# Order of the even mixer's projection and of its gates, a place of its own for the attention output, and new plans for two side jobs

## What is computed

```python
def even_mixer(x, w_in, w_out, lam_params, sub_g, lb, hg_g, lam_init, cos, sin):
    h = x @ w_in
    qa, ka, va, hq, hf, hi, hg = jnp.split(h, cuts, axis=-1)
    o_a = diff_attention(qa, ka, va, lam_params, sub_g, lam_init, cos, sin)
    o_b = hgrn2(hq, hf, hi, hg, lb, hg_g)
    return jnp.concatenate([o_a, o_b], axis=-1) @ w_out

def hgrn2(hq, hf, hi, hg, lb, out_g):
    q = silu(hq); f = lb + (1 - lb) * sigmoid(hf); kk = 1 - f
    ...
    o = o_intra + o_inter
    return rms_norm(o, out_g) * silu(hg)

def second_block(x, c, ctx, c_ctx, w_mod, b_mod, ...):
    mod = s_lat @ w_mod[i] + b_mod[i]        # per layer, needs no x
    mod_c = s_ctx @ w_mod[i] + b_mod[i]
```

## Time and profile before

| what | value |
|---|---|
| median of 3 runs | 1862.49 us (1861.61 to 1865.78) |
| the profiled execution | 1861.59 us, span 1860.3 us |
| TensorE (PE) busy | 1791.5 us, 96% |
| VectorE (DVE) busy | 1274.8 us, 69% |
| ScalarE (ACT) busy | 990.7 us, 53% |
| HBM read | 331.55 MB, 179 GB/s over the span |
| mean granted TensorE clock | 0.987 |

### The profile page before, as it was taken

One profiled execution on the slowest core, in us unless ns is written; L12 is line 12 of the kernel. 1 busy time (PEld: TensorE's weight loads), 2 busy tenths in 40 slices (PEclk: granted clock), 3 DMA queues, 4 the chain that ended last, 5 costly groups with the idle time before them and its releaser, 6 DMA issues. The chain is left out here.

```text
span 1860.3 us, 35694 instructions
## 1 busy us (share of the span) xinstructions
PE 1791.5 (96%) x14792; PEld 1666.0 (90%) x14792; DVE 1274.8 (69%) x2351; ACT 990.7 (53%) x1740; POOL 77.5 (4%) x78
## 2 busy tenths in 40 slices
PE   7999999999999999999999999999999999989997
PEld 6877799978988999999899988899999888779997
DVE  5556566667778855876666777766667867876665
ACT  4563544455656644654665655544456564644443
POOL 0000100020000100000200101000001000100000
PEclk9999999999999999999999999999999999999999
DMA  9878866765434465455454443455555543235653
GB/s 377 307 269 315 327 187 189 223 223 164 132 130 133 155 187 188 131 164 182 138 172 159 144 163 103 148 165 181 188 193 185 167 136 103 81 120 185 183 185 121
DMA packets 93825, 334.92 MB, mean 180 GB/s; under 512 B 10960, under 2 KB 12880, under 8 KB 93536
## 3 DMA queue, kind: packets, MB, share of 16 engines
q1 hardware_dynamic: 92016, 327.33, 53.9%
q0 software_dynamic: 1648, 5.31, 0.9%
HBM read 331.55 MB, written 1.05 MB: 179 GB/s over the span
## 5 line engine op out<-in xcount | busy, mean ns | idle before, releaser
L565 DVE TENSOR_TENSOR low<-ring,high 128x1024 fp32r<-128x1024 f32 x410 | 503.6, 1229 | 218.8 <-ACT high L557 206.7
L590 PE MATMUL bank<-XHx,high 128*128 128x256 f32 x2096 | 609.5, 291 | 26.1 <-DVE low L565 10.0
L591 PE MATMUL bank<-XLx,high 128*128 128x256 f32 x2096 | 593.7, 283 | 0.0
L592 PE MATMUL bank<-XHx,low 128*128 128x256 f32 x2096 | 592.8, 283 | 0.0
L557 ACT CAST high<-ring 128x1024 fp32r<-128x1024 f32 x410 | 428.4, 1046 | 280.8 <-PE bank L592 227.7
L590 PEld LDWEIGHTS bank<-XHx,high 128*128 128x128 f32 x2096 | 399.8, 191 | 42.9 <-issue 18.3
L591 PEld LDWEIGHTS bank<-XLx,high 128*128 128x128 f32 x2096 | 400.3, 191 | 1.3
L592 PEld LDWEIGHTS bank<-XHx,low 128*128 128x128 f32 x2096 | 400.1, 191 | 0.0
L590 PE MATMUL bank<-XHc,high_side 128*128 128x256 f32 x608 | 180.7, 297 | 1.2 <-DVE low_side L565 1.2
L591 PE MATMUL bank<-XLc,high_side 128*128 128x256 f32 x608 | 171.4, 282 | 0.0
L592 PE MATMUL bank<-XHc,low_side 128*128 128x256 f32 x608 | 171.2, 282 | 0.0
(11 more groups left out here) (448 smaller groups left out, 3054.7 us busy)
## 6 DMA issues: line engine op xcount, KB each, us to landing
ring<-in_stream SPq DMA_DIRECT2D x410, 512.0 KB, 3.7
ring_side<-in_stream SPq DMA_DIRECT2D x110, 512.0 KB, 3.7
ring_mod<-in_stream SPq DMA_DIRECT2D x96, 512.0 KB, 7.2
x_nb<-in_rpb POOLq DMA_DIRECT2D x6, 256.0 KB, 3.5
x_late_NB<-in_rpb POOLq DMA_DIRECT2D x6, 256.0 KB, 3.2
Xx<-in_x SPq DMA_DIRECT2D x2, 512.0 KB, 5.7
Xc<-in_ctx SPq DMA_DIRECT2D x1, 1024.0 KB, 7.1
out<-y SPq DMA_DIRECT2D x8, 128.0 KB, 2.0
```

The costliest lines, as they stand in the source:

```text
L565: nc.vector.tensor_tensor(st.low[:, j % st.n_ring, :], st.ring[:, j % st.n_ring, :], st.high[:, j % st.n_split, :].bitcast(F32), ALU.subtr ...
L590: nc.tensor.matmul(out, wh, xh, start=(i == 0), stop=False)
L591: nc.tensor.matmul(out, wh, xl, start=False, stop=False)
L592: m = nc.tensor.matmul(out, wl, xh, start=False, stop=(c == ks[-1]))
```

## The change

It does these things. `da_o` moves out of the group of buffers whose place the recurrence's buffers take over. The projection goes hf, hv, hq, hg instead of hq, hg, hf, hv; the copies likewise. The gates go sigmoid of hf (with lb's ahead of it), silu of hq, silu of hg. The split of the mixer's output waits for the product of column 27 instead of the last of hv. The recurrence's decays wait for the attention's last values instead of the attention half's split. Both plans get other numbers.

```diff
--- before.py
+++ after.py
@@ -351,10 +351,10 @@
                 self.hq, self.hf, self.hg = (sb(s, "even_" + n, 4, SEQ) for n in ("hq", "hf", "hg"))
                 self.HV = sb(s, "even_hv", NQ, 512)
                 self.c["causal"] = sb(s, "c_causal", 512)
+                self.da_o = sb(s, "da_o", HEADS_E, SEQ)
                 with ExitStack() as t:
                     self.eq, self.ek, self.eV = sb(t, "even_q", 4, SEQ), sb(t, "even_k", 4, SEQ), sb(t, "even_v", NQ, 512)
                     self.da_T, self.da_PT = sb(t, "da_scores", 2, 1024), sb(t, "da_turned", 2, 512)
-                    self.da_o = sb(t, "da_o", HEADS_E, SEQ)
                 with ExitStack() as t:
                     lf, kk, b, qi, ki, qo, ks = [flat(self.hf)] + [
                         sb(t, f"hgrn_{n}", HEADS_E * SEQ)[:, :] for n in ("k", "sum", "q_in", "k_in", "q_out", "k_out")]
@@ -1509,14 +1509,14 @@
     nc, A = k.nc, k.A
     A.wait_ge(k.s_exps, (yield "da", "exp", HEADS_E - 1))
     lb = k.px.small[:, 56:60]
-    for name, buf, func, col in (("hq", k.hq, ACT.Silu, 15), ("hg", k.hg, ACT.Silu, 27), ("hf", k.hf, ACT.Sigmoid, 19)):
+    A.wait_ge(k.s_vec, (yield "lb", "difference"))
+    for name, buf, func, col in (("hf", k.hf, ACT.Sigmoid, 19), ("hq", k.hq, ACT.Silu, 15), ("hg", k.hg, ACT.Silu, 27)):
         for i in range(col - 3, col + 1):
             A.wait_ge(k.s_copied, (yield "ev", "copied", i))
         k.tables("silu" if func == ACT.Silu else "sigmoid")
+        if name == "hf":
+            nc.scalar.activation(lb, lb, ACT.Sigmoid).then_inc(*A.tick(k.s_act, 0.3, ("lb", "sigmoid")))
         nc.scalar.activation(flat(buf), flat(buf), func).then_inc(*A.tick(k.s_act, A_us(1024), (name, "ready")))
-    A.wait_ge(k.s_vec, (yield "lb", "difference"))
-    k.tables("sigmoid")
-    nc.scalar.activation(lb, lb, ACT.Sigmoid).then_inc(*A.tick(k.s_act, 0.3, ("lb", "sigmoid")))
 
 
 def hgrn_part(k, half):
@@ -2179,9 +2179,12 @@
     for col in range(2, 8):
         yield from one("ev", col, "ev_w_in", 0, col, range(DC), moving_x(k, w, x))
     yield from rows("evV", 0, "ev_w_in", [8, 9, 10, 11], x)
-    for col in [*range(12, 16), *range(24, 28), *range(16, 20)]:
+
+    for col in range(16, 20):
         yield from one("ev", col, "ev_w_in", 0, col, range(DC), moving_x(k, w, x))
     yield from rows("evV", 2, "ev_w_in", [20, 21, 22, 23], x)
+    for col in [*range(12, 16), *range(24, 28)]:
+        yield from one("ev", col, "ev_w_in", 0, col, range(DC), moving_x(k, w, x))
     for i in range(DC):
         yield from one("ev out", i, "ev_w_out", 0, i, range(DC), moving_x(k, w, lambda c: ("mixed", "ev", c)), free="added")
     for layer in range(DEPTH):
@@ -2412,8 +2415,8 @@
         return self.late if self.done() < due else self.rank
 
 
-MOD_PLAN = [(0, 0), (440, MOD_TILES)]
-SIDE_PLAN = [(480, 0), (830, 33), (1300, 92), (1520, 110)]
+MOD_PLAN = [(0, 0), (120, 16), (200, 48), (385, 72), (440, MOD_TILES)]
+SIDE_PLAN = [(480, 0), (840, 35), (1300, 94), (1530, 110)]
 
 
 def emit(k):
@@ -2441,7 +2444,7 @@
     chunks = lambda buf, n: [buf[:, i, :] for i in range(n)]
     qk = list(enumerate(chunks(k.eq, 4) + chunks(k.ek, 4)))
     jobs = [(i, dst, QSCALE if i < 4 else 1.0, ACT.Copy) for i, dst in qk]
-    more = [(col + i, buf[:, i, :], 1.0, ACT.Copy) for col, buf in ((12, k.hq), (24, k.hg), (16, k.hf)) for i in range(4)]
+    more = [(col + i, buf[:, i, :], 1.0, ACT.Copy) for col, buf in ((16, k.hf), (12, k.hq), (24, k.hg)) for i in range(4)]
     v_rows = [(i, k.eV[:, i, :], 1.0, ACT.Copy) for i in range(2)] + [(2 + i, k.HV[:, i, :], 1.0, ACT.Copy)
                                                                      for i in range(2)]
     k.add(A, scalar_copies(k, "ev", after_first(jobs + more, [])), 1)
@@ -2460,14 +2463,14 @@
     k.add(T, tensor_rms(k, x, "da rms", 2, 512, k.c["mean128"][:, :]), 0)
     k.add(A, scalar_rms(k, x, "da rms", o, [[("da", "stored", 1), ("hf", "ready")], [("da", "stored", 3)]], 0, rs), 0)
     k.add(V, vector_rms(k, "da rms", o, lambda i: x.small[:, 53:54], None, rs), 0)
-    free = [("evV", "product", 3)]
+    free = [("ev", "product", 27)]
     high, low = ([b[:, s, :] for s in pairs] for b in (x.XH, x.XL))
     k.add(A, scalar_mixed(k, "da rms", o, high, free), 0)
     k.add(V, vector_mixed(k, "da rms", o, high, low, [[("mixed", "ev", 0), ("mixed", "ev", 1)],
                                                       [("mixed", "ev", 2), ("mixed", "ev", 3)]]), 0)
     for half in range(2):
         tag = ("hgrn", half)
-        k.add(V, vector_hgrn_decays(k, half, [("mixed", "ev", 3)]), 0)
+        k.add(V, vector_hgrn_decays(k, half, [("da", "values", 3)]), 0)
         k.add(A, scalar_hgrn_decays(k, half), 0)
         k.add(T, tensor_hgrn(k, half), 0)
         k.add(V, vector_hgrn(k, half), 0)
```

## The result

The changed kernel takes 1853.91 us (median of 4 runs, 1851.73 to 1855.4), the kernel before 1862.05 (4 runs, 1860.77 to 1865.78): 8.1 us less. The ratio of the runs is 0.9948, with a 95% interval of 0.9935 to 0.996. The median lies 0.1 us outside the range given, on the fast side. The profiled execution is the slowest of the four, 1855.4 us with a span of 1854.1.

A forecast was written before the change was run, and what follows sets the result against it. TensorE was taken as the bound, busy 1791.5 of 1860.3 us, leaving only idle and clock. Terms 2.7 + 0.8 - 1.9 - 3.7 + 0 = -2.1 on 1861.6 gave 1859.5, plus 0.9 for the median: 1860.4 us; range 1854 to 1867.5.

The forecast's parts named there:

- second layer norm: At the second layer norm, a batch now fills 1.93 of PE's 2.72 us wait for the normed chunk: -1.9 us.
- odd mixer's start: Ahead of the odd mixer's rows, a batch fills 1.93 of a 2.75 us wait and avoids the low clock: -3.7 us.
- second block: From 480 us on, side work dealt anew by the changed SIDE_PLAN was expected to cost +0 us.
- The mixer's end: After the even mixer's projection, 8.8 us on ACT against 4.9 on PE: a 3.9 us gap with low clock, +2.7 net.
- one modulation batch (L724, 1.93) and the 12 matmuls on the four chunks: At the mixer's end, part of the PE work counted behind the projection's last matmul, 4.9 us in all.
- the gap at the mixer's end does not open: Rival at the even mixer's end: the 5.7 us shrink to what was there before or less, 1855.4 us; chance 0.22.
- Inside the recurrence: In the even mixer, recurrence steps among products wait for ACT copies: +0.8 us, between bounds of nothing and 3 us.
- The clock that fell there cost nothing: At the second layer norm, the low clock behind the 2.72 us wait gives nothing back, since the next chunks were late.
- The rival of the batches coming late: In the layer norm, batches land too late and its 1.9 us gain is lost: 1862.3 us; chance 0.15.
- The side plan: In the second block, two plan numbers move by two tiles: +0 us, -5 for one place less, +11 for two more.
- count of near places: In the second block, side tiles used up in 24 matmuls: three such places before, three and one nearly one after.
- The table load: On ACT at the mixer's end, each load costs 1.30 us; the skill's 2.66 would make the sum about 1863.2.

The follow-up runs named there:

- a1: The changed kernel itself, run again beside other variants: 1853.92 us, 0.9954 of the kernel before; its profiled execution has a span of 1849.6 us.
- e5: The changed kernel with the old MOD_PLAN alone: 1859.97 us, 0.9972 of the kernel before.
- e1: The kernel before with the new MOD_PLAN alone: 1863.95 us, 1.0002 of the kernel before.
- s1: The changed kernel with SIDE_PLAN's second entry (850, 36) instead of (840, 35): 1864.19 us, 1.0009 of the kernel before.
- g1: The changed kernel with the planner's figure for a side tile's landing 3 us longer: 1880.13 us, 1.0097 of the kernel before.
- e3: The changed kernel with the old SIDE_PLAN alone: 1864.09 us, 1.0 of the kernel before.
- e4: The kernel before with both new plans, MOD_PLAN and SIDE_PLAN, its mixer's order unchanged: 1868.27 us, 1.0019 of the kernel before.
- s2: The changed kernel with SIDE_PLAN entries (850, 37), (1300, 96), (1540, 110): 1864.81 us, 1.0013 of the kernel before.
- g3: The kernel before with the planner's figure for a side tile's landing 3 us longer: 1886.31 us, 1.0123 of the kernel before.

## Why the prediction was wrong

The predicted time was 1860.4 us, with no difference that can be told as the likeliest case; the measured one is 1853.9, clearly faster. Point by point, from the two profiles (the first part here takes in the low clock behind the odd mixer's gap, 1.7 us, which the split above counts to the second, and the moved work has a row of its own):

| term | forecast | measured |
|---|---|---|
| mixer's end and recurrence | +2.7 + 0.8 | -2.2 (first norm 4.1 us earlier, of it 1.9 for one batch fewer) |
| first layer norm | none | -2.8 (gap 3.06 to 1.22, clock about 1) |
| second layer norm | -1.9 | -2.5 (idle 4.07 to 3.16, clock 1.6) |
| odd mixer's start | -3.7 | -4.4 (gap 2.74 to 0, clock 1.7) |
| side products and a turn, now behind the first L629 | none | -1.3 |
| sum of the first part | -2.1 | -13.2 (the starts give -11.2 - 1.7 = -12.9) |
| second block | 0 | +6.6 in the first profile, +2.3 in a1's (with the 1.3 moved to it) |

- **The step that failed first is "The mixer's end".** Its term was +2.7 us. Its chain on ACT was right to 0.1 us, its cover on PE was misread: "one modulation batch (L724, 1.93) and the 12 matmuls on the four chunks" are a batch, the 12 matmuls, the statistics and a second batch. With 6.7 us of cover (8.75 less the two waits) instead of 4.9 the gap is 2.1 in the forecast's sum and 2.03 in the trace, in two pieces, and the low clock didn't come (e5, with one batch as cover, has both). The sign of the term hung on this one row: PE is idle for 2.16 us where it was idle for 2.96, and at full clock. A turn fewer is some 0.3 us of the -2.2; the rest is PE busy for less on the same work, and was not followed. The prediction had given the case that "the gap at the mixer's end does not open" 0.22, and 1855.4 us; it came nearest, but for reasons that the trace doesn't show: ACT's queue ran as in the forecast, and what filled the gap was the second batch.
- **Inside the recurrence** +0.8 was forecast for waits beside products. The stretch from 120 to 158 us has 2.16 us idle in all (38.00 less 35.84 in the windows), of which 2.03 are the two waits behind the projection: the lower bound, nothing, was right.
- **The first norm was left out**, as the order there was the same. The order doesn't say when a load lands; the wait for p's had a size of its own. It was 1.8 us shorter in this profile, and the low clock behind it was gone: 2.8 us together.
- **The second norm and the odd mixer** went as forecast, each a bit better. That "The clock that fell there cost nothing" was wrong: from 409.37 to 413.09 PE's products stand 0.64 us apart by threes, against 0.35 at full clock, and this is gone. The rival of the batches coming late did not happen in the changed kernel: no L724 waits there for its tiles (in e1 one does, 0.56 us at 140 us), with the queues at 408 GB/s from 392 to 403 us.
- **The side plan** at "+0, with -5 and +11" was the right range for a wrong reason. The count of near places has no hold on it (s1, g1). Second parts that are 12 to 15 us longer than before do exist (e3, e4, s1, s2), but of their side tiles' waits only e4's have grown (17.5 and 4.0 us in all, against 8.4 and 3.7 before; e3 12.1, s1 10.5). The change escapes them by its choice of numbers.
- **The nearness of the total is luck.** The first part was off by 11 us, and the second block gave 2 to 7 of them back, for which the prediction had no term.
- **The table load**: 1.28 us and 1.30 to the next, twice more, at 150.79 and 153.42. By the Trainium skill (ScalarE: Activation LUTs, section What ACT_TABLE_LOAD costs), with some 1380 ns of DRAIN for each, the chain would have been 11.5 us and not 8.75, an estimate; the trace again has no such time.

## What to carry to other kernels

In a queue that is made by a planner, price an edit by the stretches that it leaves alone as well: here the first 440 us gained 11 us, and a change of one or two tiles in a plan moved the other 1420 by 7 to 10. Split every profile at a point that ends equal work before explaining a total, count what stands ahead of it in both, and run the plan's numbers each by itself. Take a second profile of the same kernel before explaining a difference of a few us between two. Where a forecast hangs on what covers a chain, find the end of the last producer in the order by counting products from a known place, since 12 equal rows of one product look like 12 of the next.

## What the runs showed of the hardware

That a wait of 2.7 us brings the low clock, and 1.6 us doesn't, held in the profile of the kernel before and not beyond it. In e1 the first norm's wait was 1.64 us (its row is above), and the 4 us from 192 on were granted 0.57:

```profile
192.00:196.00 4.00, 3.87 (x13) 0.57 1.04 417
```

In s1 PE waited 3.36 us for a side tile, and the clock behind it was full:

```profile
965.49 0.36 PE L590 MATMUL bank<-c_hidden_high,high_side 128*128 128x256 f32 x1 [3.36 <-DVE low_side L565]
```

```profile
965.50:969.50 4.00, 4.00 (x34) 1.00 0.03 11
```

The same place can go both ways. The kernel before and g3 have the same instructions up to the end of the mixer, and PE waits 1.61 us there in the one and 1.60 in the other; these are the 4 us behind the wait, in the kernel before and in g3:

```profile
162.00:166.00 4.00, 4.00 (x35) 1.00 0.98 386
```

```profile
162.20:166.20 4.00, 4.00 (x22) 0.60 0.98 386
```

The 1.02 us wait of the changed kernel's two profiles, shown above, is a second such pair. So the length of the last wait alone doesn't tell, and what else counts was not tried. A drop of the clock in one profile is therefore one draw, and a term of 1.6 us that rests on it may not be there in the next execution.

The second surprise is the spread itself: the same program, in two profiles, agrees to 0.2 us over its first 428 us and differs by 4.3 us over the rest. Nor is the first part always that steady. Up to L629 the instructions of e3 are those of the changed kernel, and those of g3 are the ones of the kernel before; they reach it at 428.8 and at 441.4 us, 1.0 and 2.3 us later.
